# Dense products of a three-block network as one 32-bit product each, with one weight ring of nine slots

## The reference

```python
x = first_block(x, c, ...)    # mod = silu(c) @ w_ada; h @ w_in; window attention and
                              # a gated recurrence; @ w_out; router; 32 experts, top 4
x = second_block(x, ...)      # @ w_in_2; two recurrences; @ w_out_2;
                              # gated feed-forward with a convolution; a gate product
return third_block(x, ...)    # swiglu, gated MLP over chunks, swiglu, swiglu,
                              # sparse attention (nsa), swiglu; a layer norm after each

def swiglu(x, w_in, w_out):   # D_MODEL = 1024, D_FF = 2816
    a, b = split(x @ w_in); return (silu(a) * b) @ w_out
```

## Time and profile before

| | us |
|---|---|
| median of 3 runs | 2871.69 (2868.49 to 2873.08) |
| the profiled execution, first to last instruction | 2868.7 |
| TensorE matmul busy | 2694.3 (94%), 16538 instructions |
| TensorE weight load busy | 1872.1 (65%) |
| VectorE busy | 1369.0 (48%) |
| ScalarE busy | 940.1 (33%) |
| read from memory | 709.93 MB |

### The profile page before, as it was taken

One profiled execution on the slowest core, in us unless ns is written; L12 is line 12 of the kernel. 1 busy time (PEld: TensorE's weight loads), 2 busy tenths in 40 slices (PEclk: granted clock), 3 DMA queues, 4 the chain that ended last, 5 costly groups with the idle time before them and its releaser, 6 DMA issues. The chain is left out here.

```text
span 2868.7 us, 39672 instructions
## 1 busy us (share of the span) xinstructions
PE 2694.3 (94%) x16538; PEld 1872.1 (65%) x16538; DVE 1369.0 (48%) x1957; ACT 940.1 (33%) x1243; POOL 222.2 (8%) x160
## 2 busy tenths in 40 slices
PE   8878999999999999968899999999999999999998
PEld 6653323333233332267699789899889899898897
DVE  3562221322212222276677655666575665664755
ACT  4342111111111111044454443444344443425433
POOL 2100000000000000000000010054020010102200
PEclk9888999999999999977899999999999999989999
DMA  9538999999999999932255555455556456441453
GB/s 310 204 131 332 418 416 414 381 417 417 417 416 382 407 416 417 406 117 89 92 180 188 176 183 192 149 188 186 166 194 196 151 201 202 146 151 31 161 195 114
DMA packets 292703, 713.64 MB, mean 249 GB/s; under 512 B 15587, under 2 KB 189369, under 8 KB 259430
## 3 DMA queue, kind: packets, MB, share of 16 engines
q1 hardware_dynamic: 281168, 690.27, 64.8%
q10 hardware_dynamic: 9734, 17.02, 1.8%
q0 software_dynamic: 1616, 3.74, 0.4%
HBM read 709.93 MB, written 1.05 MB: 248 GB/s over the span
## 5 line engine op out<-in xcount | busy, mean ns | idle before, releaser
L374 DVE TENSOR_TENSOR lo<-ring,hi 128x2048 fp32r<-128x2048 f32 x251 | 600.6, 2397 | 305.2 <-ACT hi L365 305.1
L1824 PE MATMUL bank<-expert,xg 128*64 128x512 f32 x2176 | 508.6, 601 | 23.3 <-DMA expert<-in_w_mlp 22.4
L365 ACT ACTIVATE hi<-ring 128x2048 fp32r<-128x2048 f32 x251 | 475.7, 1897 | 156.6 <-PE bank L643 125.7
L435 PE MATMUL bank<-x_hi,hi 128*128 128x256 f32 x1568 | 382.8, 284 | 0.0
L435 PE MATMUL bank<-x_lo,hi 128*128 128x256 f32 x1568 | 380.3, 281 | 0.0
L1824 PEld LDWEIGHTS bank<-expert,xg 128*64 128x64 f32 x2176 | 142.6, 136 | 314.1 <-issue 268.8
L435 PEld LDWEIGHTS bank<-x_hi,hi 128*128 128x128 f32 x1568 | 295.1, 188 | 3.3 <-issue 1.6
L435 PEld LDWEIGHTS bank<-x_lo,hi 128*128 128x128 f32 x1568 | 295.5, 188 | 2.5 <-issue 1.0
L1921 DVE TENSOR_TENSOR acc<-bank,acc 128x512 f32<-128x512 f32 x136 | 84.5, 684 | 425.7 <-PE bank L1911 425.6
L1894 PE MATMUL bank<-expert,aT 128*64 128x512 f32 x1088 | 243.9, 597 | 2.7 <-DMA expert<-in_w_mlp 2.3
L440 PE MATMUL bank<-x_hi,lo 128*128 128x256 f32 x1568 | 204.0, 282 | 0.0
(11 more groups left out here) (622 smaller groups left out, 3828.9 us busy)
## 6 DMA issues: line engine op xcount, KB each, us to landing
expert<-in_w_mlp SPq DMA_DIRECT2D x384, 1024.0 KB, 16.9
ring<-in_l_ffn_w_in SPq DMA_DIRECT2D x88, 1024.0 KB, 5.1
ring<-in_l_ffn_w_out SPq DMA_DIRECT2D x44, 1024.0 KB, 4.8
ring<-in_w_ada SPq DMA_DIRECT2D x24, 1024.0 KB, 6.9
ring<-in_l_gm_w_in SPq DMA_DIRECT2D x24, 1024.0 KB, 5.2
ring<-in_ffn_w_up SPq DMA_DIRECT2D x22, 1024.0 KB, 5.1
ring<-in_w_in SPq DMA_DIRECT2D x21, 1024.0 KB, 5.5
ring<-in_l_gm_w_out SPq DMA_DIRECT2D x12, 1024.0 KB, 4.9
```

Source lines behind the costliest of these rows:

```text
L365: e.activation(k.half("hi", u), k.slot(j), ACT.Copy).then_inc(*k.up("hi_done"))
L374: e.tensor_tensor(k.half("lo", u), k.slot(k.units[u][0]), k.half("hi", u).bitcast(F32), SUB).then_inc(*k.up("lo_done"))
L435: e.matmul(o, l, r, start=fresh, stop=False, skip_group_check=True)
L1824: i = e.matmul(banks[n][j][h * CAP:(h + 1) * CAP, :], x, W[:, (2 * h + j) * 512:(2 * h + j + 1) * 512], start=c == 0, stop=False, skip_gro ...
```

## The change: what it does

All splits go: `split_act`, `split_dve`, `parts_act`, `parts_dve`, `upper_act`, `lower_dve` and their tiles. The dense products read the weights straight from the ring and the activations as F32, one product where there were three. The activation's chunks after a norm are written by ScalarE (banks 0 and 2) and VectorE (banks 1 and 3) in parallel. `hi`, `lo` and the separate expert tile become one ring of nine slots; a slot is free once its unit's last matmul is done (`unit_done`), for w_ada, dense units and experts alike. SP no longer waits for the end of block 1's dense products before it loads the first expert, and loads nine slots ahead after the experts. Gate results have three tiles `tmp0` to `tmp2` in block 3.

```diff
-NSLOT = 3
-NP = 3
+NSLOT = 9
...
 def loads_sp(k, e, begin, end):
-    for j in range(begin, end):
-        src, a, b, _, _ = k.loads[j]
-        if j >= NSLOT:
-            _, _, _, flag, key = k.loads[j - NSLOT]
-            e.wait_ge(*(k.lo_at(key) if flag == "lo_done" else k.at(flag, *key)))
-        e.dma_start(k.slot(j), src).then_inc(k.sem(f"landed{j % NSLOT}"), 16)
+    for u in range(begin, end):
+        if u >= NSLOT:
+            e.wait_ge(*k.used(u - NSLOT))
+        e.dma_start(k.weights(u), k.loads[u][0]).then_inc(k.sem(f"landed{u % NSLOT}"), 16)
...
-def unit_mm(k, e, bank, u, xhi, xlo, tok=(), parts=None):
-
-    _, kk, n, _ = k.units[u]
-    hi, lo = k.half("hi", u), k.half("lo", u)
+def unit_mm(k, e, bank, u, x, tok=()):
+
+    _, kk, n = k.loads[u]
+    w = k.weights(u)
     fresh = True
-    e.wait_ge(*k.hi_at(u))
+    e.wait_ge(*k.landed(u))
     for c in range(kk):
-        if parts and c % 2 == 0:
-            e.wait_ge(*k.dve(parts, "lo", c // 2))
-        for o, l, r in products(k, bank, hi[:, c, :], n, (xhi[:, c, :], xlo[:, c, :]), tok):
-            e.matmul(o, l, r, start=fresh, stop=False, skip_group_check=True)
+        for o, l, r in products(k, bank, w[:, c, :], n, x[:, c, :], tok):
+            m = e.matmul(o, l, r, start=fresh, stop=c == kk - 1, skip_group_check=True)
             fresh = False
-    e.wait_ge(*k.lo_at(u))
-    for c in range(kk):
-        for o, l, r in products(k, bank, lo[:, c, :], n, (xhi[:, c, :],), tok):
-            t = e.matmul(o, l, r, start=False, stop=False, skip_group_check=True)
-    t.then_inc(*k.USED())
+    m.then_inc(*k.USED(u))
...
 def ffn3_act(k, e, nm, ln):
     ups, downs = k.ffn3[nm]
     for i in range(NFF):
-        s = k.t[f"tmp{i % 2}"]
-        split_act(k, e, ups[i][0] + 3)
-        if i >= 2:
-            e.wait_ge(*k.dve((nm, i - 2), "lo", 0))
+        if i >= 3:
+            e.wait_ge(*k.used(downs[i - 3]))
         e.wait_ge(*k.used(ups[i][0]))
-        e.activation(flat(s), k.got(nm, i, 0)[:, :], ACT.Tanh, scale=0.5).then_inc(*k.ACT(nm, "tanh", i))
-        split_act(k, e, ups[i][1] + 3)
-        e.wait_ge(*k.dve(nm, "s", i))
-        if i >= 2:
-            e.wait_ge(*k.used(downs[i - 2]))
-        parts_act(k, e, (nm, i), s, k.t[f"act_hi{i % 2}"])
-        if i:
-            split_act(k, e, downs[i - 1] + 3)
+        e.activation(flat(k.t[f"tmp{i % 3}"]), k.got(nm, i, 0)[:, :], ACT.Tanh, scale=0.5).then_inc(*k.ACT(nm, "tanh", i))
...
 def experts_sp(k, e):
-    e.wait_ge(*k.lo_at(k.last_dense))
-    e.wait_ge(*k.used(k.last_dense))
```

More of the change, by code:

```diff
@@ L273, in unit, with weights, expert, landed @@
     def unit(self, name, src, a, b):
[L274 to L311, removed]
+        self.first.setdefault(name, len(self.loads))
+        self.loads.append((src, a, b))
+    def weights(self, u):
+        src, a, b = self.loads[u]
+        return self.t["ring"][0:src.shape[0], u % NSLOT, 0:a * b].rearrange("p (a b) -> p a b", a=a)
+    def expert(self, m):
+        return self.expert_base + m
+    def landed(self, u):
+        return self.sem(f"landed{u % NSLOT}"), 16 * (u // NSLOT + 1)
     def used(self, u):
         return self.sem("unit_done"), u + 1
-    def USED(self):
+    def USED(self, u):
+        if "unit_done" in self.counts and self.counts["unit_done"].n != u:
+            raise ValueError(f"load {u} out of order")
         return self.up("unit_done")
@@ L498, in value_dve, with chunks_act @@
[L498 to L519, removed]
+def chunks_act(k, e, nm, gain, bias, dst, banks=(0, 2)):
+    for i in banks:
+        e.wait_ge(*k.mm(nm, "turn", i))
+        for j in range(2):
+            c, src = 2 * i + j, k.got(nm, "turn", i)[:, j * 256:(j + 1) * 256]
+            inc = k.ACT(nm, "out", c, frees=(nm, "turn", i) if j else None)
+            if gain is None:
+                e.activation(dst[:, c, :], src, ACT.Copy).then_inc(*inc)
+            elif bias is None:
+                e.activation(dst[:, c, :], src, ACT.Copy, scale=gain[:, c:c + 1]).then_inc(*inc)
+            else:
+                e.activation(dst[:, c, :], src, ACT.Identity, bias=bias[:, c:c + 1], scale=gain[:, c:c + 1]).then_inc(*inc)
@@ new lines, in chunks_dve @@
+def chunks_dve(k, e, nm, gain, bias, dst, banks=(1, 3)):
+    for i in banks:
+        e.wait_ge(*k.mm(nm, "turn", i))
+        for j in range(2):
+            c, src = 2 * i + j, k.got(nm, "turn", i)[:, j * 256:(j + 1) * 256]
+            inc = k.DVE(nm, "out", c, frees=(nm, "turn", i) if j else None)
+            if gain is None:
+                e.tensor_copy(dst[:, c, :], src).then_inc(*inc)
+            elif bias is None:
+                e.tensor_scalar(dst[:, c, :], src, gain[:, c:c + 1], None, MUL).then_inc(*inc)
+            else:
+                e.tensor_scalar(dst[:, c, :], src, gain[:, c:c + 1], bias[:, c:c + 1], MUL, ADD).then_inc(*inc)
@@ L1474, in mixer_out_act @@
     t = k.t
-    parts_act(k, e, "mo_parts", t["o"], t["mo_hi"])
-    for g in range(4):
-        split_act(k, e, k.first["w_out"] + g + 3)
     add_normed_act(k, e, "post1", lambda b, h: k.got("w_out", "acc", b, h)[:, :], sums_done(k, "w_out"))
@@ L1491, in mixer_out_dve @@
     rms_dve(k, e, "pre2")
-    for c in range(4, KC):
-        if c % 2 == 0:
-            e.wait_ge(*k.mm("pre2", "turn", c // 2))
-        value_dve(k, e, "pre2", t["s2"], t["mod"][:, 24:32], c, "pre2", "out", c)
+    chunks_dve(k, e, "pre2", t["s2"], t["mod"][:, 24:32], t["x"])
 def lay_start(k):
-    with ExitStack() as c:
-        k.sb("expert", [128, NEXP, SLOT], F32, c)
     k.sb("ring", [128, NSLOT, SLOT])
-    k.sb("hi", [128, NP, SLOT], F32R)
-    k.sb("lo", [128, NP, SLOT], F32R)
     k.sb("count", [128, 1], I32)
@@ L2630, in conv_ffn_dve @@
         add(b, h)
-    lower_dve(k, e, "ple", None, None, t["f2_hi"], t["f2_lo"])
-    for g in range(4):
-        split_dve(k, e, k.first["ple_gate"] + g + 3)
+    chunks_dve(k, e, "ple", None, None, t["f2"])
     for b, h in quarters():
@@ L2694, in lay_block2 @@
             k.sb(f"cv{i}", [128, 2, 2, 256], F32, c3)
-            k.sb(f"cs{i}", [128, 2, 256], F32, c3)
-        k.first["cf"] = len(k.units)
+        k.first["cf"] = len(k.loads)
         k.cf_up, k.cf_down = swiglu_units(k, A["ffn_w_up_2"][0], A["ffn_w_down_2"][0])
@@ L3529, in nsa_act @@
             job_parts_act(k, e, x - 3)
-    for g in range(4):
-        split_act(k, e, k.first["nsa_out"] + g + 3)
     meet(k, e, ACT_, "nsa")
@@ L3539, in nsa_dve @@
         short_dve(k, e, n, 0)
-    for x in range(jobs + 3):
+    for x in range(jobs + 2):
         if x < jobs:
@@ L3548, in nsa_dve @@
             job_gate_dve(k, e, x)
-        if x >= 3:
-            job_parts_dve(k, e, x - 3)
-    for g in range(3):
-        split_dve(k, e, k.first["nsa_out"] + g + 3)
     meet(k, e, DVE_, "nsa")
@@ L3731, in program_sp @@
 def program_sp(k, e):
-    loads_sp(k, e, 0, k.last_load)
+    after = k.expert(12 * NE)
+    loads_sp(k, e, 0, k.expert_base)
     experts_sp(k, e)
-    e.wait_ge(*k.expert_free(max(m for m in range(12 * NE) if m % NEXP < NSLOT)))
-    loads_sp(k, e, k.last_load, k.last_load + NSLOT)
+    loads_sp(k, e, after, after + NSLOT)
     overflow_sp(k, e)
-    loads_sp(k, e, k.last_load + NSLOT, len(k.loads))
+    loads_sp(k, e, after + NSLOT, len(k.loads))
     out_sp(k, e)
```

464 lines of the change are left out of this document (140 added, 324 removed).

## The result

The median went from 2872.4 us (2868.5 to 2876.0, four runs) to 3065.3 us (3062.7 to 3067.9, four runs): ratio 1.0666, 95% interval 1.0649 to 1.0682. Slower, as forecast, but by 193 us and not by 237: the time lies 44 us under the forecast and 14 us under the range's lower end. The profiled execution of after spans 3066.1 us, the slowest of its four; before's, 2868.7 us, was the fastest of its four. Between the two profiles the change is +197 us, so some 4 us of the 44 are which executions were profiled, and 40 us are to be explained.

A forecast was written before the change was run, and what follows sets the result against it. TensorE was taken to bound the dense stages, loads the experts, with TensorE gaps in the recurrences. Dearer products, +277 us, less 40 won back, gave +237 on 2868.7, with 3 for the median 3109 us; range 3079 to 3143.

The forecast's parts named there:

- What bounds the kernel: Whole kernel: TensorE bounds the dense stages, the 384 loads bound the experts, and TensorE has gaps in the two recurrences.
- The price of a product: Dense units: a plain product costs 1.19 and 1.22 times its three passes, +183 us column, +102 us row units.
- The weight load: Dense products: a record's weight load (0.19 us) fits under the record before it.
- rival 4: Dense products: the weight load is not hidden, 0.2 us more each, +990 us; chance 0.01.
- rival 3: Dense products: a plain product needs fewer passes, -470 us, some 2360 us in all; chance 0.02.
- Four odd units, -8: A 16-column unit, a 48-column unit and two half token-by-token units: -2 us each, -8 us together.
- Won back in block 2's recurrence, 17 us: Recurrence of block 2: of 27 us that TensorE waited for hS and z, 17 us come back.
- Rival 2: TensorE's listed waits: all 50 us won back, plus 20 us of half clock, 3079 us; chance 0.08.
- Won back in block 1, 18 us: Mixer of block 1: split waits, half the w_ada load wait and some 3 us of half clock return, 18 us.
- Seams, 5 us: Places where an activation is split between stages: single waits of 2.2 and 1.4 us and similar ones go, 5 us.
- Its test: Profile after: TensorE's waits for hS, z, S, g and w_out's split fall from 39 to about 13 us.
- Rival 1: Recurrences: bound by their own arithmetic, nothing won back, TensorE's longer units add in full, 3149 us; chance 0.08.

## Why the prediction was wrong, point by point

- **What bounds the kernel.** Right for the dense stages and the experts: their stretch from 300 to 1200 us has 874.6 us of TensorE and 410 GB/s in after, as in before. In the recurrences I read TensorE's waits, one step back, and stopped there.
- **The price of a product.** Right: 6.9 us a column unit for 6.88, 6.87 a row unit for 6.84. From block 2's feed-forward to the end the kernel lost 243.4 us for about 245. The Trainium skill, "TensorE: Matmul & The Clock Gate", Back-to-back issue gap: its N/2.4 + 2.5 ns gives 216 ns for 512 columns, and the plain record of 256 columns starts every 215.8 ns. That is the page's figure for a single matmul; the trace agrees if a plain record streams its 256 columns twice. The wider loss that the prediction worked out from it for the split pass did not come, as it chose.
- **The weight load** is hidden (rival 4 fell), and no record is cheaper than the rows said (rival 3 fell).
- **Four odd units, -8.** Mis-sized: the mixed unit of block 2 alone went from 15.5 to 7.2 us, the 48-column unit from 8.3 to 3.6. I had priced them without looking at their own time and clock. The row that I did read was misread: the 0.213 us of a 48-column pass is its price at the lower clock, not at full speed (last section).
- **Won back in block 2's recurrence, 17 us: the step that failed.** The sum put block 2's mixer at +15 us of dearer products and -18 us won back, with the seam. It measured -34.3 us, so on the sum's own terms 49.5 us were won back. The gaps gave 29 us (31.6 to 2.8), not 17 of 27, and the clock and the short passes gave the rest: the small products at L839 took 21.4 us in before and 14.7 in after, and its dense column products together 85.0 and 85.9 (both from the starts of TensorE's records), where the sum had 10 more. Rival 2 was the nearest, "everything is won back" with 20 us of half clock, and I gave it 0.08; its 3079 us are still 14 over. What misled me was to share the waits out between splits and arithmetic by what stood in the chain at one place. The row there even carried the clue: "2.65 <-ACT hi L365", idle time of VectorE ahead of a split, as did with 305 us of it. I counted the instructions that would go and not the waits that would go with them. Put back one after the other, the work cost 11.2 us, the slots 8.5 and the place 17.0. These prices hold in that order only: shortening the splits with slots and place as they were gave 27 us. There VectorE had nine times 2.3 us less to do and waited 7.0 us less for ScalarE's half (43.4 to 36.4), so most of a wait can stay while the stage shrinks, and the sum of an engine's waits is no price either. How the three act together is not shown.
- **Won back in block 1, 18 us.** Too little by 6 to 7: splits 13.0 (209.6 to 196.6), ring 12.4 (196.6 to 184.2), 25.4 together. I had taken half of the 8.6 us of w_ada loads. With plain products and loads three ahead TensorE waits another 6.5 us for w_in, a wait that it did not have in before.
- **Seams, 5 us**: with 7.8 us between plain products with splits and after in the rest (1694.8 to 1687.0), right in kind, slightly small.
- **Its test**, waits for hS, z, S, g and the split of w_out "down from 39 to about 13 us": they fell to 1.2 us for hS and, at w_out, 1.1 us for the last attention output. This is the sign of the prediction that fails most plainly.
- **Rival 1** (nothing won back, 3149 us): plain products with splits kept measured 3139.3. Even with the splits there, the longer products did not add to block 2's mixer in full, as it says; they added 0.6 us.
- **Small slips.** The range is 3079 to 3139 by its half-range; the 3143 has no working. Rival 2's waits add up to 51.6 us, not 50. Neither matters here.

## What to carry to other kernels

When an engine waits, follow the wait back until you reach work, not just one step: here TensorE waited for VectorE, VectorE for ScalarE, and ScalarE for a unit of TensorE's, and a preparation step of two engines cost 11.2 us by its work and 25.5 more once its three slots and its late place in ScalarE's queue were added, in that order. Its place in the producer's queue is worth trying first, since it costs one number (24 us here). And price an arithmetic change stage by stage: the same edit was worth 34 us in a stage that waits and cost 243 us in stages bound by TensorE, so apply it only where the other engines are late.

## What the runs showed of the hardware

- TensorE's clock was at its lower level while TensorE was busy without a gap: 16.00 of 16.00 us at 0.50 from 1340 us on. It had been busy for 13.16 of the 15 us before, at clock 1.00:

```profile
1325.00:1340.00 15.00, 13.16 (x112) 11.76 (x110) 12.08 (x22) 8.78 (x13) 0.00 (x0) 1.00 0.41 141
```

  It also fell with no gap near. In before, around the 48-column unit:

```profile
2520.00:2549.00 29.00, 29.00 (x240) 28.14 (x240) 20.14 (x56) 8.09 (x11) 0.00 (x0) 1.00 0.53 178
2549.00:2556.00 7.00, 7.00 (x64) 6.90 (x62) 6.54 (x9) 0.40 (x2) 0.00 (x0) 1.00 0.15 57
2556.00:2558.70 2.70, 2.70 (x27) 2.70 (x25) 0.27 (x2) 2.09 (x2) 0.00 (x0) 1.00 0.55 182
2558.70:2564.60 5.90, 5.90 (x29) 5.89 (x28) 2.29 (x1) 0.07 (x1) 0.00 (x0) 0.50 0.60 215
```

  From 2549 us on TensorE ran matmuls of 60 and then 48 moving columns. So the lower level costs time without showing as a wait, here some 7 us in one unit. Whether a gap or narrow matmuls ahead of it bring it on was not isolated; the second place has only the narrow ones.
- A split pass hardly shrinks with its columns, clock for clock: at 1.00 those of 48 columns started every 0.112 us (2556.38 to 2558.62 us) and those of 256 every 0.12. The 0.213 us of the earlier trace rows are the same passes at clock 0.50. In plain form the mixed unit with 128-column records took 7.2 us in all (1310.5 to 1317.7 us), against 6.9 of a full one.
- A plain record costs 0.2158 us for 256 columns and two are needed, so 0.43 us for a product: four times 256/2.4 GHz. The Trainium skill, "FP8 and Floating Point Precision", TensorE Precision Notes, says a true 32-bit product takes four passes. The trace agrees by its time; it shows them as two records.
